# Token rows through a scratch in memory instead of one-hot matmuls, in the expert stage of a decoder trunk

## The reference

```python
def moe_ffn(x, w_router, b_router, w_gate, w_up, w_down):
    logits = (x @ w_router).astype(jnp.float32) + b_router.astype(jnp.float32)
    top_vals, top_idx = lax.top_k(logits, TOP_K)          # TOP_K = 2
    weights = jax.nn.softmax(top_vals, axis=-1)
    gates = jnp.sum(jax.nn.one_hot(top_idx, N_EXPERTS, dtype=jnp.float32) * weights[..., None], axis=-2)
    out = jnp.zeros_like(x)
    for e in range(N_EXPERTS):                            # N_EXPERTS = 8
        out = out + gates[..., e:e + 1].astype(x.dtype) * swiglu(x, w_gate[e], w_up[e], w_down[e])
    return out
```

## Time and profile before

| | |
|---|---|
| median of three runs | 1063.82 us |
| profiled execution | 1064.27 us, its span 1062.2 us |
| PE busy | 1035.2 us (97%) |
| DVE busy | 774.8 us (73%) |
| ACT busy | 636.1 us (60%) |
| POOL busy | 28.4 us (3%) |
| moved by DMA | 265.13 MB, mean 250 GB/s |

### The profile page before, as it was taken

One profiled execution on the slowest core, in us unless ns is written; L12 is line 12 of the kernel. 1 busy time (PEld: TensorE's weight loads), 2 busy tenths in 40 slices (PEclk: granted clock), 3 DMA queues, 4 the chain that ended last, 5 costly groups with the idle time before them and its releaser, 6 DMA issues.

```text
span 1062.2 us, 15010 instructions
## 1 busy us (share of the span) xinstructions
PE 1035.2 (97%) x5836; PEld 942.4 (89%) x5836; DVE 774.8 (73%) x778; ACT 636.1 (60%) x680; POOL 28.4 (3%) x55
## 2 busy tenths in 40 slices
PE   8999999999999999999899999999999999999996
PEld 6987889999999998888798898989989899898995
DVE  4557565465456648666588898988889888898886
ACT  4655454433444545455467776877767777676864
POOL 1201000000000000000100000000000000000000
PEclk9999999999999999999599999999999999999998
DMA  9744666565563674335269899999999989899892
GB/s 317 215 145 145 206 194 207 168 208 170 176 231 120 228 179 131 128 119 204 94 238 340 320 343 349 325 345 329 346 321 341 352 326 344 328 351 346 314 349 93
DMA packets 131994, 265.13 MB, mean 250 GB/s; under 512 B 9330, under 2 KB 55426, under 8 KB 131955
## 3 DMA queue, kind: packets, MB, share of 16 engines
q1 hardware_dynamic: 130530, 259.80, 70.6%
q0 software_dynamic: 1424, 4.78, 1.4%
HBM read 263.52 MB, written 1.05 MB: 249 GB/s over the span
## 4 chain that ended last, share of the span: by engine, by line
PE 88%; DVE 6%; ACT 3%; issue 1%; DMA 1%; POOL 1%; SPq 0%; POOLq 0%; ACTq 0%; DVEq 0%
PE A L442 21%; PE A L443 21%; PE A L444 21%; PE S L442 5%; PE S L444 5%; PE S L443 5%; PE T L796 3%; DVE lo L1271 2%; PE T L487 2%; PE S L818 2%; PE T L847 1%; ACT hi L907 1%; DMA raw<-in_gm_w_in 1%; PE T L522 1%; ACT R L953 1%
## 5 line engine op out<-in xcount | busy, mean ns | idle before, releaser
L1271 DVE TENSOR_TENSOR lo<-raw,hi 128x1792 fp32r<-128x1792 f32 (+3 forms) x320 | 556.0, 1779 | 122.9 <-ACT hi L907 122.8
L907 ACT ACTIVATE hi<-raw 128x1792 fp32r<-128x1792 f32 (+3 forms) x320 | 464.8, 1503 | 189.7 <-PE A L444 153.1
L442 PE MATMUL A<-lo,xT_hi 128*128 128x448 f32 (+2 forms) x964 | 350.7, 364 | 2.4 <-DVE xT_lo L1302 2.4
L443 PE MATMUL A<-hi,xT_lo 128*128 128x448 f32 (+2 forms) x964 | 346.6, 359 | 0.0
L444 PE MATMUL A<-hi,xT_hi 128*128 128x448 f32 (+2 forms) x964 | 346.5, 359 | 0.0
L442 PEld LDWEIGHTS A<-lo,xT_hi 128*128 128x128 f32 x964 | 181.7, 188 | 17.7 <-DVE xT_lo L1302 3.0
L444 PEld LDWEIGHTS A<-hi,xT_hi 128*128 128x128 f32 x964 | 181.5, 188 | 15.7
L443 PEld LDWEIGHTS A<-hi,xT_lo 128*128 128x128 f32 x964 | 181.7, 188 | 14.7
L442 PE MATMUL S<-lo,xT_hi 128*128 128x512 f32 x224 | 88.7, 396 | 0.0
L444 PE MATMUL S<-hi,xT_hi 128*128 128x512 f32 x224 | 87.5, 391 | 0.0
L443 PE MATMUL S<-hi,xT_lo 128*128 128x512 f32 x224 | 87.2, 389 | 0.0
(11 more groups left out here) (197 smaller groups left out, 991.0 us busy)
## 6 DMA issues: line engine op xcount, KB each, us to landing
raw<-in_moe_w_gate SPq DMA_DIRECT2D x32, 1792.0 KB, 9.0
raw<-in_moe_w_up SPq DMA_DIRECT2D x32, 1792.0 KB, 9.3
raw<-in_moe_w_down SPq DMA_DIRECT2D x32, 1792.0 KB, 9.4
raw<-in_ff_w_gate SPq DMA_DIRECT2D x8, 1408.0 KB, 6.2
raw<-in_ff_w_up SPq DMA_DIRECT2D x8, 1408.0 KB, 6.0
raw<-in_ff_w_down SPq DMA_DIRECT2D x8, 1408.0 KB, 6.2
raw<-in_gm_w_in SPq DMA_DIRECT2D x10, 1024.0 KB, 5.2
raw<-in_w_mem_kv SPq DMA_DIRECT2D x8, 1024.0 KB, 5.9
```

The source lines that it names most:

```text
L442: nc.tensor.matmul(out, stat[0], mov[1], start=start, stop=False)
L443: nc.tensor.matmul(out, stat[1], mov[0], start=False, stop=False)
L907: return nc.scalar.activation(out, in_, ACT.Copy)
L1271: nc.vector.tensor_tensor(piece(lo, SPLIT, u, i), piece(raw, RAW, u, i), piece(hi, SPLIT, u, i).bitcast(F32), ALU.subtract).then_inc(lo_do ...
```

## The change

The gather and scatter by one-hot matmuls inside the loop are replaced by rows in a scratch tensor `slots` in device memory: 18 blocks of 128 rows x 1024 f32 (one zero block, one block for each expert and pass, 512 KB each).

- While layer 0's dense MLP runs, SP writes zeros to the 18 blocks, one after each of 18 weight loads.
- After routing, POOL writes the normed token rows (`rows_n`, made by two more ACT copies) to their places with 4 indirect transfers of 512 KB, each row to its slot.
- The first expert's rows are still gathered by matmuls. In each pass SP loads the next expert's block into `xrow` (behind weight load 9) and PE turns it with 8 transposes (`turn_rows`). The output of the expert before is copied by ACT from the banks S to `yrow` (`output_rows`), and SP stores it over that expert's own block (behind weight load 5).
- After the last store POOL fetches the rows back with 4 indirect transfers, and DVE adds them to `h`, each times its gate (`add_rows`, 4 instructions of 1024 columns). The last expert's output is still scattered by matmuls.
- Out of the loop go: the scatter matmuls, the `sel` transposes with their ACT copies, `output_lo`, `add_outputs` and `one_hot`.

```diff
@@ block.sync @@
+            clear_after = [u for gu, dn in U_FF for u in (*[v for pair in gu for v in pair], *dn)][:BLOCKS]
             for u in range(3, U_MOE):
                 load(u, units[u][0])
+                if u in clear_after:
+                    b = clear_after.index(u)
+                    sp.wait_ge(zero_set, 1)
+                    sp.dma_start(slots[b].rearrange("p (a c) -> p a c", c=NT * P),
+                                 sel[:, :].bitcast(F32).unsqueeze(1).to_broadcast([P, D // (NT * P), NT * P])
+                                 ).then_inc(zero_in if b else y_stored, 16)
...
+                    if j == 5:
+                        for b in range(2):
+                            sp.wait_ge(s_free[b], ve + S_MOE // 2 + 1)
+                        sp.dma_start(slots[bass.ds(ve, 1)].rearrange("b p d -> p (b d)"), yrow
+                                     ).then_inc(y_stored, 16)
+                    if j == 9:
+                        sp.wait_ge(xg_in, 16 * 2 * NT)
+                        sp.wait_ge(t_done, ve * PER_T + T_MOE + 2)
+                        sp.dma_start(xrow, slots[bass.ds(ve + 2, 1)].rearrange("b p d -> p (b d)")
+                                     ).then_inc(xrow_in, 16)
@@ block.tensor @@
+            def turn_rows(tj, ve):
+
+                pe.wait_ge(xrow_in, ve * 16 + 16)
+                for b in range(2):
+                    j = tj + b
+                    pe.wait_ge(t_free[j % 2], ve * PER_T + 2 * (j // 2))
+                    for i in range(4):
+                        last = nc.tensor.transpose(T[j % 2][:, i * P:(i + 1) * P],
+                                                   xrow[:, (4 * b + i) * P:(4 * b + i + 1) * P], ident[:, :])
+                    last.then_inc(t_done, 1)
...
+            pe.wait_ge(sel_done, 2)
+            bank = s_job(S_MOE)
+            for t in range(NT):
+                last = nc.tensor.transpose(bank[:, t * P:(t + 1) * P], sel_end[:, t * P:(t + 1) * P], ident[:, :])
+            last.then_inc(sel_turned, 1)
...
                 hidden_expert(ve, (U, U + 1), A_MOE, lambda: gathered(1))
-                scatter(0, ve)
...
-                hidden_expert(ve, (U + 2, U + 3), A_MOE + 1, second_scatter)
+                hidden_expert(ve, (U + 2, U + 3), A_MOE + 1, nothing)
...
                 down(ve, U + 10, 0, 1)
-                pe.wait_ge(sel_done, ve + 2)
                 with pe.If(ve < rounds - 1):
-                    gather(t1 + 6, ve)
+                    turn_rows(t1 + 4, ve)
                 down(ve, U + 11, 1, 1)
-            scatter(0, rounds)
-            scatter(1, rounds)
+            pe.wait_ge(selT_set, 1)
+            scatter(0)
+            scatter(1)
@@ block.scalar @@
+            act.wait_ge(route_mm, 1)
+            for t in range(NT):
+                nc.scalar.activation(rows_n[:, t, :], xn[:, t, :], ACT.Copy, scale=scaled(N_FN[1], t)
+                                     ).then_inc(rows_ready, 1)
...
+            def output_rows(c, ve):
+
+                act.wait_ge(used, ve * MU + U_MOE - 1 + c)
+                if c == 0:
+                    act.wait_ge(y_stored, ve * 16 + 16)
+                act_copy(yrow[:, c * 512:(c + 1) * 512], S[(S_MOE + c) % 2][:, :]
+                         ).then_inc(s_free[(S_MOE + c) % 2], 1)
@@ block.vector @@
             with dve.Fori(0, rounds) as ve:
-                output_lo(0, ve)
-                output_lo(1, ve)
                 split(U + 2, ve)
-                add_outputs(0, ve)
                 split(U + 3, ve)
-                add_outputs(1, ve)
...
-                one_hot(ve + 1)
...
-            output_lo(0, rounds)
-            output_lo(1, rounds)
-            add_outputs(0, rounds)
-            add_outputs(1, rounds)
+            dve.wait_ge(y_back, 16 * 2 * NT)
+            for k in range(2):
+                for t in range(NT):
+                    add_rows(k, t)
+            output_lo(0)
+            output_lo(1)
+            add_outputs(0)
+            add_outputs(1)
@@ block.gpsimd @@
+            pool.wait_ge(zero_in, 16 * (BLOCKS - 1))
+            pool.wait_ge(y_stored, 16)
+            pool.wait_ge(rows_ready, NT)
+            pool.wait_ge(row_to_set, 1)
+            for k in range(2):
+                for t in range(NT):
+                    pool.indirect_dma_start(slot_rows, bass.IndirectOffsetOnAxis(row_to[:, k, t:t + 1], 0),
+                                            rows_n[:, t, :], None).then_inc(xg_in, 16)
...
+            pool.wait_ge(xg_in, 16 * 2 * NT)
+            pool.wait_ge(y_stored, rounds * 16 + 16)
+            step(nc.gpsimd.tensor_tensor(row_from[:, :, :], row_to[:, :, :], row_kept[:, :, :], ALU.mult))
+            for k in range(2):
+                for t in range(NT):
+                    pool.indirect_dma_start(y_from[k][t], None, slot_rows,
+                                            bass.IndirectOffsetOnAxis(row_from[:, k, t:t + 1], 0)
+                                            ).then_inc(y_back, 16)
```

More of the change, by code:

```diff
@@ L180, in build @@
     S_MOE = 14
+    slots = nc.dram_tensor("slots", (BLOCKS, P, D), F32, kind="Internal").ap()
+    slot_rows = slots.rearrange("b p d -> (b p) d")
     XN_OF = numbered(("x0", 4), ("mem0", 2), ("fn0", 4), ("mem1", 2), ("x1", 4), ("fn1", 4), ("final", NT))
@@ L310, in build @@
         ys = [a[:, NT * D:NT * D + D] for a in wk]
+        xrow, yrow = R1[:, 0:D], R1[:, D:2 * D]
         xn = R1[:, :].rearrange("p (t d) -> p t d", t=NT)
@@ L331, in build @@
         iota = R3[:, 3072:3072 + P]
+        sel_end = kr[:, 0].rearrange("p t s -> p (t s)")
+        rows_n = R2[:, :].rearrange("p (t d) -> p t d", t=NT)
+        y_from = [[R2[:, 0:D], R2[:, D:2 * D]], [R3[:, 2 * ECH:2 * ECH + D], GB1[:, :]]]
         qr = GB1[:, :].rearrange("p (t h r) -> p t h r", t=NT, h=HEADS)
@@ L800, in gather, with scatter @@
                     last.then_inc(t_done, 1)
-            pe.wait_ge(moe_const, 1)
-            for c in range(2):
-                pe.wait_ge(s_free[(S_MOE + c) % 2], (S_MOE + c) // 2)
-                last = nc.tensor.matmul(S[(S_MOE + c) % 2][:, :], selT[:, 0:P], ys[0][:, c * 512:(c + 1) * 512],
-                                        start=True, stop=True)
-            last.then_inc(scat_done, 1)
+            def turn_rows(tj, ve):
[7 more added lines that the diff above has]
+                    last.then_inc(t_done, 1)
             pe.wait_ge(xs_done, NT)
             pe.wait_ge(sel_done, 1)
-            gather(T_MOE, 0)
-            def scatter(t, ve):
+            gather(T_MOE)
+            pe.wait_ge(sel_done, 2)
[3 more added lines that the diff above has]
+            last.then_inc(sel_turned, 1)
+            def scatter(t):
                 for c in range(2):
                     s = S_MOE + 2 + 2 * t + c
-                    pe.wait_ge(s_free[s % 2], ve * 3 + s // 2)
+                    pe.wait_ge(s_free[s % 2], rounds * (PER_S // 2) + s // 2)
                     for n in range(2):
@@ L1219, in _ @@
             with act.Fori(0, rounds) as ve:
-                output_hi(0, ve)
-                output_hi(1, ve)
+                output_rows(0, ve)
+                output_rows(1, ve)
                 split(U + 2, ve)
@@ L1225, in _ @@
                 split(U + 4, ve)
-                for t in range(NT):
-                    j = t1 + t
-                    act.wait_ge(t_done, ve * 8 + j + 1)
-                    act_copy(selT[:, t * P:(t + 1) * P], T[j % 2][:, 0:P]).then_inc(t_free[j % 2], 2)
                 split(U + 5, ve)
@@ L1684, in _, with one_hot @@
             dve.wait_ge(a_free[j % 2], 2 * (j // 2 + 1))
-            step(nc.vector.tensor_scalar(slot_of[:, :, E:2 * E], slot_of[:, :, 0:E], -1e4 - P, None, ALU.add))
-            step(nc.vector.tensor_scalar(slot_of[:, :, 0:E], slot_of[:, :, 0:E], -1e4, None, ALU.add))
-            def one_hot(ve):
+            step(nc.vector.tensor_scalar(slot_of[:, :, :], slot_of[:, :, :], -1e4, None, ALU.add))
+            def one_hot(dst, slots):
                 for t in range(NT):
-                    last = nc.vector.tensor_scalar(sel[:, t * P:(t + 1) * P], iota,
-                                                   slot_of[:, t, bass.ds(ve, 1)], None, ALU.is_equal)
+                    last = nc.vector.tensor_scalar(dst[:, t * P:(t + 1) * P], iota, slots(t), None, ALU.is_equal)
                 last.then_inc(sel_done, 1)
@@ L1737, in _ @@
             dve.wait_ge(consts, 2)
[L1738 removed]
+            one_hot(sel, lambda t: slot_of[:, t, 0:1])
             step(nc.vector.tensor_scalar(r1[:, 7, 1:2], r1[:, 7, 0:1], P + 0.5, float(E), ALU.is_gt, ALU.mult))
             nc.vector.tensor_scalar(nround[:, :], r1[:, 7, 1:2], float(E), None, ALU.add).then_inc(route_done, 1)
+            step(nc.vector.tensor_scalar(r1[:, 8, 0:1], r1[:, 7, 1:2], -float(P) / E, None, ALU.mult))
+            step(nc.vector.tensor_scalar(slot_last[:, :], slot_of[:, :, E - 1], r1[:, 8, 0:1], None, ALU.add))
+            dve.wait_ge(t_done, T_ROPE + 3)
```

(2 more changed lines are left out.)

143 lines of the change are left out of this document (81 added, 62 removed).

## The result

The changed kernel takes 1053.48 us in the median of five runs (1050.37 to 1057.39), the kernel before 1063.46 us on the same chip (five runs, 1062.89 to 1063.83): ratio 0.9905, 95% interval 0.9882 to 0.9927. It is faster by about 10 us. The prediction said 1067.0 us, slower, so its direction was wrong; the time lies inside its range and outside the likeliest case's own.

The account below looks back on a forecast made before the run. PE bounds the kernel, transfers close behind; after the change, DMA at 358 GB/s. 1064.27 + 1.3 (transfers) + 1.4 (end) + 0.4 (transposes) = 1067.4 us, median 1067.0; range 1042 to 1081, likeliest case 1061 to 1073.

Parts of the forecast that it names:

- What PE loses: Expert loop: removed gathers, scatters and `sel` transposes save PE 34.6 us; PE could do a full pass in 60.6 us.
- What DMA gains: Expert stage: 12.6 MB more, 181.4 MB in all at 358 GB/s, take 506.7 us, +1.3 us; a pass 64.4 us.
- the ring: Rival, expert stage: three weight slots set the pace, (landing + split + wait) / 3 a unit; 67.2 us a pass, 1077 to 1081 us; 22%.
- the rate: Forecast case, expert stage: DMA holds 358 GB/s, give or take 4; 1061 to 1073 us, chance 40%.
- 365 to 376 GB/s: Rival, expert stage: transfers are more even and hold this rate; 1057 us at 365, 1046 at 376; 20%.
- the load that landed after 7.1 us: Expert stage before the change: read as a load that finds the queue empty, against a median landing of 9.3 us.
- ACT and DVE not on the path: Expert passes: ACT and DVE keep up with a unit of 5.05 us, so work they lose saves no time.
- New waits in the passes: Expert passes: SP's `output_rows` wait already met, `xrow` loads in time; PE's new wait is 0.
- Two transposes, +0.4: Ahead of the loop: two more transposes at the low clock there cost 0.4 us.
- The end: After the last pass: DVE's four additions of 1.28 us come before the second half's `lo`; +1.4 us.
- They should be: End of kernel: rows are back in time, the last store being issued half a pass or more before DVE asks.
- Signs named in advance: Changed profile: DMA share 0.98 or more, 355 to 362 GB/s, passes 64 to 65 us, landings 9.5 to 11 us.

## Why the prediction was wrong

**What PE loses: right.** 60.6 us a pass was worked out, 60.6 was measured when nothing else held PE back.

**What DMA gains: the bytes right, the step behind them wrong.** The step that failed is "the time this takes depends on one unknown, the rate that DMA can hold", taken as 351 / 0.98 = 358 GB/s. That stretch was one in which PE set the pace; the 351 was demand, and dividing by the share does not make it a capacity: share stood at 0.98 to 1.02 at 357, 370, 376, 380 and 387 GB/s. By the failed term the stage was to last 506.7 us; it lasted 491.6. That is 15.1 us of the 16.9 between the forecast's 1067.4 (for the profiled execution of before) and the 1050.5 us of the profiled execution after. The pass of 64.4 was 62.4.

**The bound itself was the ring**, which I had only as a rival, at 67.2 us a pass. The form was right (4 x (landing + split + rest)) and its two inputs wrong. I kept the rest at the 1.3 us of the kernel before; it was the slack of a ring that waits for PE, and fell to 0.5 once PE was faster. And I let the landing grow by 0.5 us; it grew by under 0.2. With 9.4, 5.7 and 0.5 the rival gives 62.4 us, which says only where its two errors lay, since the 0.5 is taken from that pass. So the two cases that I held apart, "the rate" and "the ring", had the right size in neither.

**The rival that had the number** was "365 to 376 GB/s" at 20%: the stage ran at 369, and the measured 1053.5 us lies in its span. Its reason, transfers that are more even, is not what the runs show: the rate was what the ring let through, 314 GB/s with the request later and 380 with it earlier. So its hit is luck. Its lower end was also worked out wrong: 181.4 MB at 376 GB/s take 482.4 us, so 1043 us, not 1046.

**A reading that was wrong:** the load that landed after 7.1 us did not find the queue empty. It was issued at 663.98 us, the load ahead of it landed only at 665.10, and the next was issued at 668.51, so it had company for half of its time. The figure itself stands nearly: the stage's first load, at 535.94 us and all but alone, took 7.3 us.

**ACT and DVE not on the path: half right.** They are not the bound by their own work, but their split is 5.7 us of the 15.6 us of a slot's cycle; the lever that gave 17 us was to let go of half a slot 2 us earlier.

**The zeros: right** (dense MLP 178.7 us). **New waits in the passes: right**, none of them on the chain. **Two transposes, +0.4:** the start of the stage came 1.2 us earlier; among kernels that are the same up to there it varies from 533 to 536 us, so nothing is to be read from it.

**The end: +1.4 forecast, +1.6 measured** behind the last landing. But the sentence that begins "They should be", said of the rows being back, asked only whether the reads are in time, not what they cost others: with them the last pass grew by 4.4 us, and without them it lost 4.9 us again. The prediction named this place, under the ring rival, and gave it no price of its own.

**Limits from elsewhere.** The Trainium skill (DMA: Bandwidth & Descriptors, Specifications) gives about 358 GB/s as the HBM limit per core, which is a stack's 716 GB/s divided between two cores. 370 GB/s over 374 us, and 387 over 390 us, go beyond it here, so the measurement decides: it is no ceiling for the one core of this kernel. The 408.7 GB/s of the same page's load stream (SWDGE vs HWDGE vs iDMA) was not reached in any stretch of hundreds of us. That the page's 358 equalled my 358 was chance and no support.

**Signs named in advance.** No gather in the loop, transposes at 0.87, ACT's idle time put down to weights, share of at least 0.98: as said. GB/s 370 in place of 355 to 362, and landings of 9.3 to 9.6 where 9.5 to 11 were named: the two signs that spoke against the forecast. PE "well under" the pass: it was busy 61.6 of 62.4 us. That alone told nothing, since its busy time counts the overlap with waits for weights that come a fraction late.

## What to carry to other kernels

Where a ring of buffers feeds an engine, write down a slot's cycle (landing + work until it is free + rest) and find out which of it is slack that shrinks when the engine gets faster; a busy share of DMA near 1.0 and a rate read under another bound are no capacity. A bound by a ring is cheaply told from a bound by bandwidth: ask for half of a slot as soon as that half is free, and control with the same two pieces asked for at the old time. Transfers at the end that are "in time" still cost what they add to the landing of others, and work put in front of a last link costs its full length, and more if PE's clock falls while it waits.

## What was not expected of the hardware

- Landing depends weakly on load: 9.3 us at 337 to 357 GB/s, 9.4 at 370, 10.0 at 376, and 8.3 at 314. The shortest in the six passes of the kernel before was 7.1 us, with another load in flight for half of that time; the stage's first load, all but alone, took 7.3 us.
- DMA share stood at 0.98 to 1.02 over a range of rates from 357 to 387 GB/s.
- Four indirect reads of 512 KB, issued within 6 us, lengthened down loads from 9.6 (the passes' median) to up to 13.4 us; POOL needed 0.9 to 2.6 us for each issue.
- Two more stores a pass cost 2.5 to 3.1 us, two more loads 1.9 to 2.6 us (by the medians and by the passes).
- PE's granted clock fell to 0.52 and 0.50 after 4.3 and 8.7 us of idle time, and stayed at 1.00 after 1.0 us.
